# All four 64x64 quadrants of the PE array for the triangular solve of a chunked RWKV-7 branch

## The reference, cut to what matters

```python
def step(state, inp):                       # 8 heads, state 64 x 64 per head, 512 steps
    r_t, w_t, k_t, v_t, a_t, b_t = inp
    sa = jnp.einsum('bhij,bhj->bhi', state, a_t)
    state = (state * w_t[:, :, None, :] + sa[..., None] * b_t[:, :, None, :]
             + v_t[..., None] * k_t[:, :, None, :])
    y_t = jnp.einsum('bhij,bhj->bhi', state, r_t)
    return state, y_t
_, ys = lax.scan(step, s0, (r, w, k, v, -kk, kk * a))
```

## Time and profile before

| | us |
|---|---|
| median of 3 runs | 1278.04 |
| lowest, highest | 1270.3, 1286.15 |
| profiled execution, its time | 1270.44 |
| its span in the profile | 1268.6 |
| of this the recurrence, first `forms` to last output copy | 124.7 (260.5 to 385.2) |

### The profile page before, as it was taken

The page is one execution under the profiler, slowest core; times in us unless marked ns, Lnnn a source line. Parts: engine busy times, 40 slices in busy tenths (PEclk is TensorE's granted clock), DMA queues, the critical chain, the costliest instruction groups (busy, mean ns, idle before and its releaser), DMA issues. The chain is left out here.

```text
span 1268.6 us, 17615 instructions
## 1 busy us (share of the span) xinstructions
PE 1066.7 (84%) x7777; PEld 641.7 (51%) x7777; DVE 453.0 (36%) x743; ACT 267.0 (21%) x449; POOL 150.3 (12%) x187
## 2 busy tenths in 40 slices
PE   3799999988998998999995439999888888887881
PEld 2677544478895786667674413333333333233330
DVE  3766577663532854123255511111111111111113
ACT  5532243323234234011121101011000000000000
POOL 0000000062591000000000031111111111111100
PEclk9699999999998788999998669999999999899996
DMA  8857421000003001310083819999999999999975
GB/s 321 288 206 258 141 72 61 1 5 4 4 4 133 1 17 67 132 67 31 36 317 134 350 25 406 409 408 385 407 411 408 411 412 405 418 405 410 410 296 202
DMA packets 53074, 281.63 MB, mean 222 GB/s; under 512 B 8187, under 2 KB 9413, under 8 KB 40581
## 3 DMA queue, kind: packets, MB, share of 16 engines
q1 hardware_dynamic: 46480, 268.61, 53.7%
q0 software_dynamic: 5504, 8.58, 2.1%
q10 hardware_dynamic: 1014, 3.30, 0.7%
HBM read 276.21 MB, written 12.65 MB: 228 GB/s over the span
## 5 line engine op out<-in xcount | busy, mean ns | idle before, releaser
L1621 PE MATMUL bank<-w_ring,xT 128*64 128x512 f32 x336 | 150.8, 602 | 27.2 <-DMA w_ring<-in_w 14.5
L1196 DVE TENSOR_TENSOR hid<-bank,silu_a 64x512 f32<-64x512 f32 x32 | 22.2, 693 | 257.0 <-ACT silu_a L652 257.0
L1189 DVE SCALAR_TENSOR_TENSOR mod<-bank,table,mod 64x512 f32<-64x512 f32 x64 | 47.9, 748 | 173.6 <-PE bank L1635 172.6
L1621 PEld LDWEIGHTS bank<-w_ring,xT 128*64 128x64 f32 x336 | 45.5, 139 | 123.8 <-issue 123.8
L652 ACT ACTIVATE silu_a<-bank 64x512 f32<-64x512 f32 x32 | 18.9, 591 | 408.5 <-PE bank L1622 408.5
L1621 PE MATMUL bank<-w_ab,xT 128*64 128x512 f32 x176 | 85.6, 643 | 16.5 <-DMA w_tok<-in_w 15.8
L1256 PE MATMUL bank<-x_r,ring_r 128*128 128x512 f32 x240 | 97.8, 408 | 0.1
L1635 PE MATMUL bank<-w_ring,hidT 128*64 128x512 f32 x352 | 87.2, 641 | 10.4 <-ACT hidT L656 10.4
L1622 PE MATMUL bank<-w_tok,xT 128*64 128x512 f32 x176 | 85.8, 644 | 0.0
L1285 PE MATMUL bank<-ring,hT 128*128 128x512 f32 x192 | 85.0, 595 | 0.0
L732 POOL DMA_INDIRECT y_rows<-mod,table x32 | 29.8, 930 | 429.2 <-DVE mod L1189 429.2
(11 more groups left out here) (339 smaller groups left out, 2029.8 us busy)
## 6 DMA issues: line engine op xcount, KB each, us to landing
w_ring<-in_w SPq DMA_DIRECT2D x54, 2048.0 KB, 36.0
w_tok<-in_w SPq DMA_DIRECT2D x21, 2048.0 KB, 38.6
w_ab<-in_w SPq DMA_DIRECT2D x11, 2048.0 KB, 34.3
w_qkv<-in_w SPq DMA_DIRECT2D x10, 2048.0 KB, 40.0
ring<-in_w_ada SPq DMA_DIRECT2D x8, 2048.0 KB, 8.1
ring<-in_w_in SPq DMA_DIRECT2D x7, 2048.0 KB, 8.2
tokm<-in_w_ada SPq DMA_DIRECT2D x4, 2048.0 KB, 14.9
tokm<-in_w_in SPq DMA_DIRECT2D x3, 2048.0 KB, 12.8
```

The lines of the kernel that those rows point to most:

```text
L1189: dve.scalar_tensor_tensor(ys[:, b, 512 * n:512 * n + 512], bank[5 + n][SLOTS * n:SLOTS * n + SLOTS, :], weight_of(e), gate2[:, n, :], ALU ...
L1196: dve.tensor_tensor(hid[:, :], bank[3][SLOTS:P, :], silu_a[:, :], ALU.mult).then_inc(hid_v, 1)
L1621: pe.matmul(bank[2][0:SLOTS, :], xT[:, b, k, :], w1[:, k, :], start=(k == 0), stop=(k == KT - 1))
```

## The change

PSUM's eight banks become four pairs (`banks[k][:, b, :]`), so that one read of VectorE or ScalarE can take from two banks. `FLIPPED[n]` says for each of the four heads of a group whether, at level `n`, its product is written to the other chunk's partitions (and to the second bank of the pair); `TURNED[n]` says the same of the transposed inverse. Two of four heads are crossed at each level, and `alternating` orders them one straight, one crossed, so that four consecutive matmuls lie in four quadrants. The tiles `INV` and `INVT` become one tile `INVS` with slots. The number of matmuls and their sizes are the same.

`m0` on VectorE becomes three instructions for each group, in place of one: two heads in place, and two heads with the two chunks' partitions exchanged. `gh` and `q` become one event `ghq` (`gains`), so that the `w` times queries products no longer wait for VectorE's `g`.

The state part is regrouped. `chain` and `next_state` work on four heads at a time (two instructions of VectorE in place of one), `outputs` is split into `within` (the two products that need no state, for both chunks of a pair at once, in four quadrants) and `from_state`. The order in a half is `within(0)`, [chain 0, from_state 0], chain 1, `within(1)`, from_state 1, chain 2, forms(1,0), from_state 2, chain 3, forms(1,1), from_state 3, forms(1,2), forms(1,3) (forms and chain 3 in the first half only).

```diff
-                        elif ev[0] == "p":
-                            mm = pe.matmul(b_[rows, at], tt_, inv, start=True, stop=True)
-                        elif ev[0] == "n":
-                            mm = pe.matmul(a_[rows, at], invt, pp, start=True, stop=True)
+            def level_p(half, k, n):
...
+                for i in alternating(FLIPPED[n]):
+                    flip, at = FLIPPED[n][i], CH * place(FLIPPED[n], i)
+                    for c in range(2):
+                        mm = pe.matmul(banks[k][half_of(c ^ flip), flip, at:at + CH], FORMS[k][half_of(c), 0, i, :], INVS[k][half_of(c), inv_slot(n - 1, i), :],
+                                       start=True, stop=True)
+                mm.then_inc(solve_mm[k], 1)
...
+        FLIPPED = {1: (1, 1, 0, 0), 2: (0, 1, 1, 0), 3: (0, 0, 1, 1), 4: (1, 0, 0, 1), 5: (1, 1, 0, 0), 6: (0, 0, 0, 0)}
...
-                            ins = dve.tensor_tensor(INVT[k], FORMS[k][:, 0], bc4("level0_t"), ALU.mult)
+                            level0_t = const("level0_t").unsqueeze(1).to_broadcast([P, 2, CH])
+                            dve.tensor_tensor(INVS[k][:, 6:8, :], FORMS[k][:, 0, 2:4, :], level0_t, ALU.mult)
+                            for c in range(2):
+                                ins = dve.tensor_tensor(INVS[k][CH - CH * c:P - CH * c, 4:6, :], FORMS[k][CH * c:CH * c + CH, 0, 0:2, :], level0_t[CH * c:CH * c + CH], ALU.mult)
...
-            def next_state(half, n):
...
-                    dve.tensor_tensor(new, bank[2 * n][to, :].rearrange("p (g n) -> p g n", g=2), HH_OF[n // 2][to], ALU.add).then_inc(chain_v, 1)
+                for g in range(2):
...
+                        dve.wait_ge(chain_mm, 2 * at - 1 + g)
+                        dve.tensor_tensor(new, chain_bank(n, g)[to, 0:256], add, ALU.add).then_inc(chain_v, 1)
```

More of the change, by code:

```diff
@@ L547, in _ @@
                         a_, b_ = bank[2 * k], bank[2 * k + 1]
-                        act.wait_ge(solve_mm[k], mm_at(half, "gh" if ev == "h" else ev))
+                        act.wait_ge(solve_mm[k], mm_at(half, "ghq" if ev == "h" else ev))
                         if ev == "x":
@@ L1343, in forms @@
                 if half:
-                    pe.wait_ge(chain_v, k + 1)
+                    pe.wait_ge(chain_v, 2 * (k | 1) + 2)
                     pe.wait_ge(out_a, k + 1)
@@ new lines, in solved @@
+            def solved(half, k):
+                pe.wait_ge(solve_a[k], a_at(half, "m5"))
+                for i in range(4):
+                    for c in range(2):
+                        r = half_of(c)
+                        pe.matmul(bank[2 * k + 1][r, P * i:P * i + HD], INVS[k][r, invt_slot(5, i), :], tok(half, k, i, c, 3), start=True, stop=True)
+                    for c in range(2):
+                        r = half_of(c)
+                        mm = pe.matmul(bank[2 * k + 1][r, P * i + HD:P * i + P], INVS[k][r, invt_slot(5, i), :], XX[k][r, i, :], start=True, stop=True)
+                mm.then_inc(solve_mm[k], 1)
@@ new lines, in gains @@
+                        pe.matmul(a_[half_of(c), at], WU[k][half_of(c), i, 0:HD], tok(half, k, i, c, 1), start=True, stop=True)
+                    for c in range(2):
+                        pe.matmul(b_[half_of(1 - c), at], tok(half, k, i, c, 1), WU[k][half_of(c), i, HD:P], start=True, stop=False)
+                    for c in range(2):
+                        pe.matmul(a_[half_of(c), 256 + CH * i:256 + CH * i + CH], WU[k][half_of(c), i, 0:HD], FORMS[k][half_of(c), 2, i, :], start=True, stop=True)
@@ L1399, in solve_step @@
+                    for c in range(2):
+                        mm = pe.matmul(b_[half_of(1 - c), at], tok(half, k, i, c, 2), tok(half, k, i, c, 0), start=False, stop=True)
                 mm.then_inc(solve_mm[k], 1)
@@ L1420, in outputs, with from_state @@
+            def from_state(half, n):
+                at, rows = 4 * half + n, half_of(n % 2)
+                pe.wait_ge(chain_v, 2 * at)
                 for k in (2 * (n // 2), 2 * (n // 2) + 1):
@@ L1461, in _ @@
-                for n in range(4):
-                    if 0 < 4 * half + n < NCH - 1:
-                        chain(half, n)
-                    outputs(half, n)
-                    if half == 0 and n:
-                        forms(1, n - 1)
-                if half == 0:
+                for k in range(NG):
+                    turn_forms(half, k)
+                for k in range(NG):
+                    keyed_values(half, k)
+                for n in range(1, 6):
+                    for k in range(NG):
+                        level_p(half, k, n)
+                    for k in range(NG):
+                        level_nm(half, k, n)
@@ new lines, in _ @@
+                for k in range(NG):
+                    solved(half, k)
+                for k in range(NG):
+                    gains(half, k)
+                within(half, 0)
+                if half:
+                    chain(half, 0)
+                    from_state(half, 0)
+                chain(half, 1)
+                within(half, 1)
+                from_state(half, 1)
+                chain(half, 2)
+                if half == 0:
+                    forms(1, 0)
+                from_state(half, 2)
@@ L1468, in _ @@
+                if half == 0:
+                    chain(0, 3)
+                    forms(1, 1)
+                from_state(half, 3)
+                if half == 0:
+                    forms(1, 2)
                     forms(1, 3)
```

199 lines of the change are left out of this document (104 added, 95 removed).

## The result

The changed kernel is slower: 1283.47 us, median of 20 runs (1274.55 to 1289.65), against 1272.78 us for the kernel before, median of 20 runs on the same chip (1267.45 to 1286.15). The ratio is 1.0071, 95% interval 1.0045 to 1.0098, which is +9 us (+6 to +12). The forecast was -3.4 us. In absolute terms it was 1275 us, but this rested on 1278.04 us for the kernel before, the median of three runs; twenty runs put that kernel 5 us lower. The prediction took 2% as the least difference that can be told; twenty runs of each tell 0.7%. The profiled execution took 1279.78 us, its span is 1278.0. Some executions of a kernel are disturbed and slower: the ratios leave them out, and of e3 and e8, whose profiled execution was such a one, only the durations of `m0` are read.

The account below looks back on a forecast made before the run. PE bounds the recurrence's levels at 29.2 ns a pass; with four quadrants, instruction supply would, at 26 to 27. Terms -4.4 + 3 + 1 - 1 - 2 = -3.4 us took 1278.0 to 1274.6 us, range 1266 to 1283.

Parts of the forecast that it names:

- (b): Masks m0: three VectorE instructions for one in each group cost +3 us (0 to +10).
- rival (3): m0 held up by GpSimd at each instruction (+10), blocks at 3.9 us (+2): +10 in all, 1288 us; chance 0.09.
- (a): Levels, p1 to m5: four quadrants, limited by instruction blocks at 3.45 us, give -4.4 us (-6.6 to +2.4).
- rivals (1): Instruction supply doesn't bind; levels go by dependence, 3.5 us against 5.66: -21 us, 1257 us; chance 0.17.
- (4): Quadrants don't overlap in this order or with two banks, passes stay at 29 ns: +1, 1279 us; chance 0.05.
- (c): Merged event ghq: VectorE's q starts only behind the last g, +1 us (-1 to +4).
- (d): State part, first half: four quadrants and moved within(0) save, masks pile up; net -1 us (-2 to +1).
- (e): State part, second half: fewer passes in the chain at 1.2 GHz, -2 us (0 to -4).
- (f): Cover: ScalarE's two-bank copies change nothing; GpSimd's rotation isn't met by a second half shorter by up to 10 us.
- Rival (2): Starved PE's clock falls to 1.2 GHz in the levels, which lose their gain: about +16, 1294 us; chance 0.08.

Follow-up runs that it names:

- e3: Kernel before with m0 in three instructions a group, each on its own partitions, no exchange; ratio 1.0044.
- e8: Kernel before with GpSimd held until m0 is done in each half; ratio 0.9976.
- e4: Changed kernel with level products of only two of the four heads of a group, results wrong; 1259.41 us, ratio 0.9890.
- e5: Changed kernel with every level matmul 32 columns wide in place of 64, same instruction count, results wrong; 1285.22 us, ratio 1.0110.
- e13: Changed kernel with one m0 instruction a group reading its matrix from PSUM (64 more passes a half), gh and q apart, GpSimd free; 1260.78 us, ratio 0.9909.
- e12: Kernel before with the state part of the change alone, GpSimd free; 1262.99 us, ratio 0.9927.
- e1: Changed kernel with one m0 instruction a group, without the exchange of partitions, results wrong; 1271.54 us, ratio 0.9993.
- e7: Changed kernel with GpSimd held for m0 as in e2, and gh and q as two events again; 1269.00 us, ratio 0.9963.
- e2: Changed kernel with GpSimd's squares held until m0 of the first half and its rotation until m0 of the second; 1273.32 us, ratio 0.9985.
- e10: e7 again, in more rounds, against the kernel before; 1269.83 us, ratio 0.9974.
- e11: Kernel before with the state part of the change alone and GpSimd held until m0 is done; 1267.27 us, ratio 0.9941.
- e6: Changed kernel with two straight heads first, then two crossed, in place of alternating; 1282.44 us, ratio 1.0080.

## Why the prediction was wrong

**The step that failed is (b), the price of `m0`.** I took +3 with +10 as the bound, by asking which row the new instructions would be like, and chose one with an input in PSUM. `m0` has both inputs in SBUF. The row that applied was the one cited beside it, L946 with 414 to 1489 ns: an instruction alone takes 0.35 us (e8), and what it has above that is time behind GpSimd. Tripling the instructions then triples the times that one must wait. Measured: +12.9 us, over the bound, since each that follows the first waits for a GpSimd instruction (0.7 to 1.4 us each in the second half). The bound itself was too low: +5 a half is twelve at the first half's mean of 0.69 us, less the 2.76 of before, and not at the slower of L946. At the second half's mean (3.55 / 4 = 0.89 us) twelve are 10.6 us, +7 for that half, and both halves together come to +12.6. That this meets the measured sum is luck in part, as the halves are off in both directions (8.3 and 10.6 us against 6.2 and 12.4). "If each of the twelve is held up" was rival (3), with the right mechanism and a chance of 0.09; it should have been the forecast. Its 1288 us comes near the measured time by another sum, as its other half, blocks at 3.9 us, did not happen. The forecast's range ended at +5 us, though its own bounds add up to +17.

**(a) was right in mechanism**: -5.6 us for -4.4, bursts of 15 to 16 ns, restarts 3.46 us apart where 3.3 to 3.5 were forecast, levels of 4.2 to 6.3 us, around 5. (The levels before were 5.0 to 5.9 us, with VectorE idle for 3.6 to 4.1, a little more than the one difference of 5.66 that I read.) e4 and e5 show that instruction count sets the time, neither columns nor dependence; rivals (1) and (4) are out. What was missing is what comes after: in the profile levels and gains together take 78.2 us against 78.4, and in e13 against e12 77.6 and 76.7. My reading is that a stage that uses instructions as fast as they come leaves none for the next one; no run tests this by itself. Of the 5.6 us, 1.2 go with the long `m0`: in e1, the changed kernel with masks of the old length, the levels give 4.4 us, the forecast's number. That the wait in `m0` lets PE's instructions pile up ahead would explain the difference, but is only argued.

**(c) was mis-sized**: +1 taken, +4 the bound, +5.4 measured. Some 2.8 us come with the denser levels (e7, with two events, still has 33.3 us of gains against 30.5 before). The rest is the merged event: e2 has 36.1 us, nearly all of the difference in the second half. I had said that PE's wait on `g` which goes was hidden. It was, and the order that it forced was useful: it put passes under VectorE's `q`, which now has 66 beside it in the second half (110 before, 142 in e7).

**(d) and (e)** gave more: -1.9 for -1, -4.5 for -2, the latter just outside its range. By themselves (e12) they are -1.5 and -6.0, because PE then also keeps 2.4 GHz in the last stage, where it had 0.52 of it before and 0.75 in the changed kernel. The clock stood in (e) as a condition of the old trace; that moving work changes it was not considered. e12 shows the gains 1.6 us shorter too in the first half, with the same code; I leave that open.

**(f)** held: no wait for the rotation in the changed kernel. Held back by the time of `m0` it is late (e7). That may be why e10 gains 3 us by its ratio where its recurrence is 7 us shorter; e11, held as well, gains 7.5 of its 8, so the hold's price is not settled.

**Rival (2)**, the clock, happened in part: 1.2 GHz from 335.8 to 349.5, in the long `m0` and behind it, and from 277.8 to 281.2, though the level stretches as a whole kept 0.92 and 0.86. In the levels it cost little, as 115 passes in 3.4 us are 29.6 ns each, against 27 by the supply; e5 says the same. Before the levels of the first half the clock was low too (0.62 from 268.4 to 276.2), and `x` took 3.5 us in place of 2.0, but PE was done with it and with `p1` by 274.7, before VectorE was with `m0` at 276.2, so this part of the rival cost nothing. Outside the recurrence nothing moved that I can put down to the change; of +9 us in the runs, 6.3 are placed, and the rest lies within what untouched stages vary.

The sum again with measured terms: -5.6 + 12.9 + 5.4 - 1.9 - 4.5 = +6.3.

## What to carry to other kernels

Before an elementwise instruction is split, look at what its operands are in and who runs beside it: its price is the neighbour's instruction for each piece, not its own size. When an engine's instruction supply binds, count instructions over the whole run of stages; here a denser stage only moved the gap. Merging two events can empty an engine under another's long stretch, and lower its clock for what follows; of this change the state part alone was worth taking, 9 us.

## What was not expected of the hardware

- VectorE's instructions with two inputs in SBUF went in lock-step with GpSimd's: 0.30 us alone, 1.03 us for each beside the rotation, and 0.35 us for a twice as large one whose matrix is in PSUM, beside GpSimd.
- TensorE's instructions come in blocks of 16 KB, here one each 3.46 us at the full pace, for 128 float32 passes with their weight loads. The Trainium skill, "Runtime: NRT & Kernel Launch", section Instruction fetch mechanics, gives the same block of 256 instructions, and says that crossing into the next is mostly hidden. With quadrants in parallel it isn't here: a gap of 1.0 to 1.3 us at each block of the first half's levels.
- At 1.2 GHz, four quadrants with 32 columns take 27 ns a pass without a gap (e5), as long as with the gaps at 2.4 GHz; the supply hides the lower clock.
- The order of straight and crossed heads within eight matmuls makes no difference that the time shows (e6).
